# Two transformer blocks on one core: first FFN pair by tokens instead of weights, and a reordered end of the experts' spill pass

## What is computed

```python
h2 = rmsnorm(x, ffn_norm_g); x = x + (silu(h2 @ w_gate) * (h2 @ w_up)) @ w_down          # block 1, D_FF 2816
x = layer_norm(ALPHA * x + mix); ffn = (silu(x @ w1) * (x @ w3)) @ w2                     # block 2, layer 0, 2816
x = layer_norm(ALPHA * x + ffn)
logits = x @ router_w + router_b; top 2 of 8 experts, gates by softmax                    # block 2, layer 1
out = sum_e gate[:, e] * (silu(x @ w1[e]) * (x @ w3[e])) @ w2[e]                          # D_FF 1408
x = layer_norm(ALPHA * x + out)
```

## Time and profile before

| | us |
|---|---|
| median of three runs | 1448.28 |
| the profiled execution's own time | 1444.18 |
| its span, first to last instruction | 1442.4 |
| TensorE busy (share of the span) | 1380.3 (96%) |
| VectorE busy | 1015.1 (70%) |
| ScalarE busy | 796.4 (55%) |
| mean granted TensorE clock | 0.991 of full |

### The profile page before, as it was taken

The page is one execution under the profiler, slowest core; times in us unless marked ns, Lnnn a source line. Parts: engine busy times, 40 slices in busy tenths (PEclk is TensorE's granted clock), DMA queues, the critical chain, the costliest instruction groups (busy, mean ns, idle before and its releaser), DMA issues.

```text
span 1442.4 us, 20488 instructions
## 1 busy us (share of the span) xinstructions
PE 1380.3 (96%) x8197; PEld 1213.9 (84%) x8197; DVE 1015.1 (70%) x1018; ACT 796.4 (55%) x802; POOL 80.3 (6%) x93
## 2 busy tenths in 40 slices
PE   6998999999999989999999999999999999999995
PEld 5986899998988878999989888788888888888884
DVE  5887545467456776454674567778888888888896
ACT  4674454454555444544544554346677767677772
POOL 2000000000000000000000000029100000000000
PEclk9999999999999999999999999999999999999998
DMA  9544566674544346666745544469999999999991
GB/s 265 160 147 125 153 189 174 180 225 132 173 164 143 125 146 187 192 174 179 224 137 168 161 146 125 146 229 325 374 359 345 338 360 357 345 358 371 355 324 37
DMA packets 238851, 317.99 MB, mean 220 GB/s; under 512 B 10544, under 2 KB 141744, under 8 KB 238640
## 3 DMA queue, kind: packets, MB, share of 16 engines
q1 hardware_dynamic: 234048, 300.52, 63.2%
q0 software_dynamic: 4720, 16.32, 3.9%
HBM read 314.70 MB, written 2.10 MB: 220 GB/s over the span
## 4 chain that ended last, share of the span: by engine, by line
PE 83%; DVE 9%; ACT 4%; issue 1%; DMA 1%; POOL 0%; SPq 0%; DVEq 0%; ACTq 0%
PE ps L1715 25%; PE ps L1717 24%; PE ps L1716 24%; DVE w_lo L1042 2%; ACT w_hi L612 1%; PE ps L2073 1%; PE ps L2092 1%; PE ps L2310 1%; DMA lg_all<-in_decay_bwd_dram 1%; DVE x L1085 1%; DVE small L1060 1%; PE ps L1756 1%; DVE x L1084 1%; PE ps L2268 1%; DMA raw<-in_w_in_dram 1%
## 5 line engine op out<-in xcount | busy, mean ns | idle before, releaser
L1042 DVE TENSOR_TENSOR w_lo<-raw,w_hi 128x2048 fp32r<-128x2048 f32 x129 | 294.8, 2290 | 190.3 <-ACT w_hi L612 162.9
L1715 PE MATMUL ps<-xt_hi,w_hi 128*128 128x256 f32 x912 | 258.4, 283 | 0.9 <-DVE xt_lo L1091 0.8
L1716 PE MATMUL ps<-xt_lo,w_hi 128*128 128x256 f32 x912 | 258.0, 283 | 0.0
L1717 PE MATMUL ps<-xt_hi,w_lo 128*128 128x256 f32 x912 | 258.0, 283 | 0.0
L612 ACT ACTIVATE w_hi<-raw 128x2048 fp32r<-128x2048 f32 x101 | 192.1, 1907 | 104.4 <-PE ps L1717 100.8
L1715 PEld LDWEIGHTS ps<-xt_hi,w_hi 128*128 128x128 f32 x912 | 174.9, 192 | 2.8 <-issue 2.0
L1716 PEld LDWEIGHTS ps<-xt_lo,w_hi 128*128 128x128 f32 x912 | 174.9, 192 | 0.9
L1717 PEld LDWEIGHTS ps<-xt_hi,w_lo 128*128 128x128 f32 x912 | 174.9, 192 | 0.0
L1591 DVE TENSOR_TENSOR w_lo<-raw,w_hi 128x2048 fp32r<-128x2048 f32 (+1 forms) x65 | 143.5, 2214 | 27.8 <-ACT w_hi L950 27.6
L1715 PE MATMUL ps<-w_hi,xt_hi 128*128 128x512 f32 (+2 forms) x432 | 156.1, 361 | 1.5 <-DVE scr L1383 1.5
L1717 PE MATMUL ps<-w_hi,xt_lo 128*128 128x512 f32 (+2 forms) x432 | 152.4, 353 | 0.0
(11 more groups left out here) (412 smaller groups left out, 2598.4 us busy)
## 6 DMA issues: line engine op xcount, KB each, us to landing
raw<-in_moe_w_dram SPq DMA_DIRECT2D x144, 512.0 KB, 5.7
raw<-in_w_in_dram SPq DMA_DIRECT2D x99, 512.0 KB, 4.9
scr<-in_moe_w_dram SPq DMA_DIRECT2D x90, 512.0 KB, 7.0
raw<-in_ffn_w_dram SPq DMA_DIRECT2D x66, 512.0 KB, 4.6
scr<-in_moe_w_dram SPq DMA_DIRECT2D x54, 384.0 KB, 5.3
raw<-in_w_gate_dram SPq DMA_DIRECT2D x22, 512.0 KB, 4.0
raw<-in_w_up_dram SPq DMA_DIRECT2D x22, 512.0 KB, 5.2
raw<-in_w_down_dram SPq DMA_DIRECT2D x22, 512.0 KB, 4.3
```

The lines of the kernel that those rows point to most:

```text
L1042: TTo(w_lo[:, slot, :], raw[:, slot, :], w_hi[:, slot, :].bitcast(F32), ALU.subtract).then_inc(lo_ready, 1)
L1715: MM(dst, a_hi, b_hi, start=start, stop=False)
L1716: MM(dst, a_hi, b_lo, start=False, stop=False)
L1717: return MM(dst, a_lo, b_hi, start=False, stop=stop)
```

## The change

Three parts. **(A)** In both FFNs the first pair is computed by `first_pair`: the tokens of a tile are the still operand, a unit's gate and up columns stream past (256 columns for each matmul, in two runs of 128 that lie 1024 floats apart), tile 0 first, then tile 1; the hidden tile comes out by rows and is turned by TensorE. The first unit is split into a place of its own (`first_unit_hi`, in the second FFN also the second unit, in `mt_hi`), so that more units are split ahead. The filler matmuls go. **(B)** In the spill pass the left half of y is finished two units earlier (`SPILL_UNITS`), scattered, added and its statistics taken before the right half; statistics of the left half are also taken after expert 7. The last norm (`last_norm`) takes only the right halves' statistics, of both tiles, before it scales. `last_scatter` starts with y's high part. **(C)** VectorE reads a spill pass's count ahead: the first before expert 7, the next at the beginning of the pass before.

```diff
+SPILL_UNITS = EXPERT_UNITS[:12] + [("D", c, part) for c, part in ((0, 0), (1, 0), (0, 1), (0, 2), (1, 1), (1, 2))]
...
+        first_unit_hi, first_unit_lo = over("first_unit_hi", scr_at, 9984, UNIT)[:, :], over("first_unit_lo", scr_at, 12032, UNIT)[:, :]
...
# ScalarE
-                    split_to(U_FFN1, w_hi[:, U_FFN1 % RING, :], U_WO + 2)
+                    split_to(U_FFN1, first_unit_hi, U_WO)
...
+            def first_pair(u0, q0, h0):
+                for t in range(TT):
+                    if t:
+                        act.wait_ge(unit_used, u0 + 2)
+                    else:
+                        act.wait_ge(ev("first_gate_up"), h0 // FT_DENSE + 1)
+                    A_(silu_t[:, t, :].rearrange("p (j n) -> p j n", j=2), ps[:, (q0 + t) % 2, :].rearrange("p (j n) -> p j n", j=2)[:, :, 0:P],
+                       ACT.Silu).then_inc(silu_ready, 1)
+                    act.wait_ge(ev("first_turned"), TT * (h0 // FT_DENSE) + t + 1)
+                    A_(h_hi_t[:, :, t * P:(t + 1) * P], ps[:, 6 + t, 0:T].rearrange("p (j s) -> p j s", j=2), ACT.Copy).then_inc(hid_hi, 1)
+                for j in (1, 2):
+                    split_hi(u0 + j + RING, (u0 + j) % RING, (u0 + j + RING) // RING + 1)
...
             take_root(1, 1)
+            split_to(U_FFN1 + 3, w_hi[:, (U_FFN1 + 3) % RING, :], U_WO + 2)
...
+                        split_to(U + 27, first_unit_hi, U + 23)
+                        take_root(n, 0)
+                        split_to(U + 28, flat(mt_hi), U + 23)
+                        take_turned(n, 0, 0)
...
# VectorE, norm(n, rms, first)
                 part(0, 0)
+                if first is not None:
+                    split_lo_to(first, first_unit_hi, first_unit_lo)
                 part(0, 1)
                 norm_head(0, rms)
                 norm_tail(n, 0, rms)
+                if first is not None:
+                    split_lo_to(first + 1, flat(mt_hi), flat(mt_lo))
+                if rms:
+                    part(1, 0)
+                    low(0, 0)
...
+            def last_norm():
+                for t in range(TT):
+                    link(part_stats(t, 1))
+                    norm_head(t, False)
+                dve.wait_ge(gb_landed, 16 * (6 + 1 + 6 - 1))
+                for t in range(TT):
+                    norm_tail(6, t, False)
...
+            def first_pair(u0, q0, h0):
+                split_lo(u0 + 2, (u0 + 2) % RING)
+                for t in range(TT):
+                    bank = (q0 + t) % 2
+                    dve.wait_ge(silu_ready, h0 + t + 1)
+                    TTo(hid[:, t, :].rearrange("p (j n) -> p j n", j=2), ps[:, bank, :].rearrange("p (j n) -> p j n", j=2)[:, :, P:2 * P],
+                        silu_t[:, t, :].rearrange("p (j n) -> p j n", j=2), ALU.mult).then_inc(hid_ready, 1)
+                    dve.wait_ge(hid_hi, h0 + t + 1)
...
+                for j in range(3):
+                    split_lo(u0 + j + RING, (u0 + j) % RING)
...
# VectorE, expert(e)
+                if e >= EXPERTS:
+                    take_hidden(2)
+                    split_moe(m + 17)
+                    take_y(0)
+                    add_moe(e, 0)
+                    add_stats(e)
+                    take_y(1)
+                    add_moe(e, 1)
...
+                    take_y(1)
                     for c in range(2):
                         add_moe(e, c)
                     split_moe(m + 20)
                     split_moe(m + 21)
+                    add_stats(e)
+                    dve.wait_ge(ev("added"), 4)
+                    dve.wait_ge(ev("added_stats"), 2)
...
+            def spilled(k, n):
                 with dve.If(n > SLOTS):
...
+                    if k + 1 < SPILLS:
+                        n = spill_count(k + 1)
                     expert(EXPERTS + k)
...
# TensorE
                 wo_part(2, 1).then_inc(unit_used, 1)
+                wo_part(3, 1, (0, 1))
                 turn_half(1, normed, 0, 0)
-                wo_part(3, 1).then_inc(unit_used, 1)
+                wo_part(3, 1, (2, 3)).then_inc(unit_used, 1)
                 turn_half(1, normed, 0, 1)
-                keep_busy(6, 14)
-                turn_rows(1, normed, [1])
...
+            def first_pair(u0, q0, norm, rows, second):
+                def gate_up(t, j, half):
+                    pe.wait_ge(lo_ready, u0 + j + 1)
+                    pe.wait_ge(xt_ready, 4 * norm + 2 * t + half + 1)
+                    for k in range(4 * half, 4 * half + 4):
+                        hi, lo = (v[:, :, k, :] for v in pairs[j])
+                        dst = ps[:, bank, j * T:(j + 1) * T].rearrange("p (a n) -> p a n", a=2)
+                        last = product(dst, xt_hi[:, k, tok], xt_lo[:, k, tok], hi, lo, k == 0, k == KT - 1)
...
+                gate_up(0, 0, 0)
+                gate_up(0, 0, 1)
+                gate_up(0, 1, 0)
+                turn_half(norm, rows, 1, 0)
+                gate_up(0, 1, 1).then_inc(ev("first_gate_up"), 1)
+                turn_half(norm, rows, 1, 1)
+                gate_up(1, 0, 0)
+                gate_up(1, 0, 1).then_inc(unit_used, 1)
+                gate_up(1, 1, 0)
+                turn_hidden(0)
+                gate_up(1, 1, 1).then_inc(unit_used, 1)
+                down_pair(s, 0, 0, start=True)
+                turn_hidden(1)
+                down_pair(s, 1, 0)
+                down_pair(s, 0, 1, start=True)
+                down_pair(s, 1, 1).then_inc(unit_used, 1)
...
                 down(16)
+                if e >= EXPERTS:
+                    last_scatter(e, 0)
                 down(17)
```

More of the change, by code:

```diff
@@ L1364, in ffn @@
                         split_lo_to(ut + 3 * i + 5, wd_hi[i + 1], wd_lo[i + 1])
-            norm(1, rms=True, ready=add_wo, after=[U_FFN1 + 2])
+            norm(1, rms=True, ready=add_wo)
             ffn(U_FFN1, Q_FFN1, H_FFN1)
@@ L1524, in mixer @@
                 return add_out
-            norm(3, ready=mixer(0), early=[U_FFN2], after=[U_FFN2 + 1, U_FFN2 + 2])
+            norm(3, ready=mixer(0), first=U_FFN2)
             ffn(U_FFN2, Q_FFN2, H_FFN2)
@@ L1691, in _, with spill_count @@
             split_moe(RING)
-            for e in range(EXPERTS):
+            def spill_count(k):
+                return dve.value_load(spill[0:1, k:k + 1], min_val=0, max_val=T)
+            for e in range(EXPERTS - 1):
                 expert(e)
-            def spilled(k):
-                n = dve.value_load(spill[0:1, k:k + 1], min_val=0, max_val=T)
+            dve.wait_ge(ev("spill_ready"), 1)
+            n_spilled = spill_count(0)
+            expert(EXPERTS - 1)
+            def spilled(k, n):
                 with dve.If(n > SLOTS):
@@ L1878, in wo_part @@
                 tok = slice(t * P, (t + 1) * P)
-                for k in range(4):
+                for k in ks:
                     w = slice(k * 512, (k + 1) * 512)
@@ L1935, in ffn_pair, with down_pair @@
                     for t in range(TT):
-                        last = down(j, t)
+                        last = down_pair(s, j, t)
                 last.then_inc(unit_used, 1)
-            def ffn(u0, q0, fresh):
-                ffn_pair(u0, (u0, q0), [(q0 + j) // 2 for j in range(2)], fresh)
+            def down_pair(s, j, t, start=False):
+                tok = slice(t * P, (t + 1) * P)
+                for c in range(2):
+                    w = slice(j * 1024 + c * 512, j * 1024 + (c + 1) * 512)
+                    last = product(ps[:, 2 + 2 * t + c, :], h_hi_t[:, j, tok], h_lo_t[:, j, tok], w_hi[:, s, w], w_lo[:, s, w], start, False)
+                return last
@@ L1941, in ffn @@
+            def ffn(u0, q0, fresh, rows, second):
+                first_pair(u0, q0, fresh, rows, second)
                 with pe.Fori(1, LOOP) as i:
@@ L2223, in _ @@
             mixer(0)
-            ffn(U_FFN2, Q_FFN2, 3)
+            ffn(U_FFN2, Q_FFN2, 3, x, (flat(mt_hi), flat(mt_lo)))
             mixer(1)
```

196 lines of the change are left out of this document (115 added, 81 removed).

## The result

| | before | after |
|---|---|---|
| median of the timed runs, us | 1448.25 | 1431.88 |
| their range | 1448.04 to 1449.43 | 1430.70 to 1432.59 |
| ratio, 95% interval | | 0.9886 (0.9872 to 0.9900) |
| profiled execution's own time | 1444.18 | 1432.59 |
| its span | 1442.4 | 1430.7 |

One more execution of the changed kernel was disturbed (3490.17 us) and is left out. From one profiled execution to the other it is only 11.6 us.

The account below looks back on a forecast made before the run. TensorE was taken as the bound, with time to win only where it waits or does filler. Gains of 6.9 + 4.2 + 1.2 = 12.3 us off the 1448.28 us median gave 1436.0 us, range 1432.0 to 1441.0.

Parts of the forecast that it names:

- The step that failed: Whole kernel: the runs' median lies 4.1 us above the profiled 1444.18 us, so the gain is taken off 1448.28.
- The sum: Whole kernel: gains of 6.9, 4.2 and 1.2 us add to 12.3 us.
- A, first block: First FFN's change-over: TensorE starts tile 0 without waiting for VectorE's norm, pair ends at 165.9; gain 6.9 us.
- A, second block: Second FFN's change-over: tile 0's groups start where filler ran, at 546.39; pair ends at 565.4, gain 4.2 us.
- B and C at expert 7: Expert 7 into the spill pass: added statistics and bare count load make the whole pass 1.3 us later; bounds 0 and 2.3.
- The end: After the spill pass: last add 1.5 us later, 2.7 us of load, statistics and waits fall away; net 1.2 us gained.
- Rival 1: New gate and up matmuls: streaming 256 columns in two runs costs double, giving 1454.5 us; chance 0.05.
- Rival 2: FFN first pairs: VectorE does not keep up, lagging 2.2 us in each FFN, giving 1440.4 us; chance 0.16.
- Rival 3: Both FFNs: tile 0's groups wait for tile 1, only 1 to 2 us left, 1446.5 us; chance 0.05.
- The clock stays at 1.00 without filler: A sign of the forecast: TensorE's granted clock stays at its upper level, 1.00, though the filler matmuls go.

Follow-up runs that it names:

- e2: The changed kernel, unchanged, timed again: 1430.71 us (4 runs), beside 1448.15 for the kernel before.
- e12: The changed kernel, unchanged, timed once more for comparison: 1430.81 us (4 runs), beside 1448.28 for the kernel before.
- e3: The changed kernel less B and C, so part A alone in both FFNs: 1435.51 us (6 runs), 12.6 us below the kernel before.
- e9: Part A alone once more, timed beside the changed kernel: 1433.28 us (4 runs), 15.0 us below the kernel before.
- e13: The kernel before with part A in the first FFN alone: 1440.01 us (5 runs), beside 1448.58, ratio 0.9945.
- e4: The changed kernel less A, so parts B and C alone: 1446.57 us (12 runs), 1.6 us below the kernel before.
- e5: The kernel before with 36 filler matmuls, twice those intended, in TensorE's 2.10 us wait at the first FFN: 1448.41 us, beside 1447.98.
- e17: The kernel before with 18 filler matmuls (9 calls) in TensorE's 2.10 us wait at the first FFN: 1448.25 us (12 runs), beside 1447.71.
- e7: The changed kernel without the two statistics behind expert 7: 1428.98 us (4 runs).
- e8: The changed kernel with the next count's load moved from the spill pass's beginning to behind its ninth low part: 1430.43 us (4 runs).
- e10: The changed kernel with part C undone, each spill pass's count read where it is needed: 1432.86 us (5 runs).

## Why the forecast was wrong

**The step that failed** is the one from the profile to the median: "the median of the runs is 4.1 us above it, and the forecast is made against the median". Taking the sum off the median supposes that these 4.1 us lie on top of every execution of the changed kernel too, though the range used them as a measure of scatter. They don't: the changed kernel's profiled execution took 1432.59 us, and of its ten other timed ones nine were shorter. For the most part the 4.1 us were falls of the clock that the profiled execution of the kernel before happened not to have: 0.991 there against 0.9877 in the mean, which is 3.0 us at 0.91 us for 0.001. With the parts as measured, 1448.25 - 13.7 = 1434.6 us would have lain within the range. The changed kernel took 1431.9, so 2.7 us of the 16.4 come from outside the parts.

How many of them are fewer falls can only be estimated. The mean clocks differ by 0.0032, but 0.0011 of that is the last stretch, where the clock costs nothing. The remaining 0.0021 are 3.0 us of clock time, 1.8 falls: 1.9 us at 0.91 us for 0.001, 2.9 us if each costs the 1.6 us of the one at 146 us. That makes 15.6 to 16.6 us, against 16.4 in the first set (interval 14.5 to 18.5) but 17.4 and 17.5 when both kernels were timed again (e2, e12). Up to 2 us of these have no place in any trace.

Whose doing the fewer falls are is only partly shown. In the change-over into the first FFN there was one in 3 of 5 profiles with its waits as they were, worth 1.6 us, and with the new first pair in none of 13. That would be 1.0 us in the mean, and it belongs to part A: the forecast priced this place from an execution in which the clock stayed up. The timed runs point the same way: part A alone gained 12.6 and 15.0 us (e3, e9) for 12.05 in the traces, e13 8.6 for 7.2, B and C alone 1.6 for 1.67 (e4). But the intervals of e3 and e13 take in the traces' values too. And taking the one wait away by filler gained nothing in e5 and e17, since the clock fell behind the next one. The rest, at 880 or 510 us for instance, comes and goes between executions in places that the change does not touch. Why it is rarer in the changed kernel at some of them and more frequent at others stays open.

**The sum** was 12.3 and the parts measured 13.7, so each term point by point:

- *A, first block, 6.9.* Measured 7.2. Allowing for the late start, TensorE turned at 144.3 and began on the first unit at 146.6, both as worked out. From there the pair took 19.1 us to 165.7 (forecast 165.9), 0.7 more than the 18.4 of its work; so of the 0.9 us of waits that the sum had, 0.7 came, in pieces that the timeline doesn't mark.
- *A, second block, 4.2.* Measured 4.85. The pair ran from 540.88 to 559.35, 18.5 us, so the 0.6 us of small waits did not come.
- *B and C at expert 7, -1.3.* The mechanism was right. The shift before the pass was 9.98 and at its first transposes 9.08, -0.9. Two sizes were off against each other: TensorE's gain at the pass's start was 0.14 and not 0.5, because it still waits 0.33 us for y's low part and once 0.16 in its issue; and its new wait is 0.81 us, not 1.8. e7 prices statistics and load together at 1.03, e8 the load at 0.65.
- *The end.* The last add came 1.1 us later, not 1.5, and the stretch behind it was 2.8 us shorter, against 2.7. I had left 0.5 us of the branch in, where the 108 ns of the Trainium skill (Advanced Engine Details and Errata, Control Flow Timing) would have let all of it go with the load. The statistics still start 0.71 us behind the last add, and e10 shows that the load was 0.64 us, so leaving it in was right: until VectorE works again the row has several times the page's figure, and the measurement decides.
- *Rival 1* (double price of two runs): 0.12 us a matmul, as one run. *Rival 2* (VectorE's lag): no wait that the timeline marks in either pair; unit 3's low part came in time. *Rival 3*: tile 0 started at once in both FFNs. *"The clock stays at 1.00 without filler"*: so it did, at both change-overs.

## What to carry to other kernels

A single profile is one draw: where the granted clock moves, compare its mean with that of the timed runs before a difference between profile and median is carried into a forecast, and compare two kernels at the same number of falls, or stage by stage from a mark of their own (at an equal clock in the stretch the parts came out within 0.1 us in all profiles that way, while medians of four executions moved by 2 us). A mean clock also counts the stretches in which TensorE is done. Filling one of several waits of the bound engine gained nothing as long as the next was still there, so look for a form that has none in the whole stretch. Count filler by the instructions that the trace shows, not by calls.

## What the runs showed of the hardware that was not expected

- The clock of TensorE fell to its lower level behind waits of 1.6 to 2.1 us between stretches of dense work, and now and then where the timeline marks no wait at all but the matmuls have 64 columns (458 us in e12, 852 us in e3), in some executions and not in others of the same kernel, each time by 1.71 us of lost clock time or a multiple of it. A fall cost 1.6 us at 146 us and 1.9 at 980, where TensorE was needed, but hardly 0.5 at 510, where it had waits behind it that took it up.
- VectorE stands idle for different times round the two branches. Not taken, into the spill pass, it is 0.20 us between the statistics and the next low part in e8; taken, past the next pass's code, 0.71 us between the last add and the statistics. The instruction's own record is 0.04 to 0.06 us in both; that the jump makes the difference is argued from these rows and not isolated. The Trainium skill (Advanced Engine Details and Errata, Control Flow Timing) has 108 ns for a compare-and-branch; the row at the end has several times as much until the engine works again.
- Reading one number from SBUF into VectorE's sequencer costs 0.64 us where nothing covers it (e8, e10), with a record of 0.32 to 0.56 us for the load itself.
